# A list scheduler that ranks ready operations by deadline: pool and gated linear attention layers on eight cores

## The reference

```python
def pool_mixer(h, w_in, w_grp, scale, w_out):
    u, z = jnp.split(h @ w_in, 2, axis=-1)
    ...
        pooled.append((cg - shifted) / cnt - uf[:, :, gi])       # trailing mean minus token
    y = jnp.einsum('blgc,gcd->blgd', t, w_grp).reshape(B, L, D_INNER)
    y = y * scale * jax.nn.silu(z)
    return y @ w_out

def gla_mixer(h, w_in, w_gate2, b_gate, head_norm, w_out):
    ...
    def step(S, inp):
        cum = jnp.cumsum(lab, axis=2)
        qe = qb * jnp.exp(cum)
        ke = kb * jnp.exp(-cum)
        att = jnp.where(mask, jnp.einsum('bhtd,bhsd->bhts', qe, ke), 0.0)
        o = jnp.einsum('bhts,bhse->bhte', att, vb) + jnp.einsum('bhtd,bhde->bhte', qe, S)
        ...
        S_new = jnp.exp(g_tot)[..., None] * S + jnp.einsum('bhsd,bhse->bhde', kd, vb)
        return S_new, o
    ...
    o = o * lax.rsqrt(jnp.mean(o * o, axis=-1, keepdims=True) + EPS)   # per-head RMSNorm
    y = o.astype(h.dtype) * jax.nn.silu(z)
    return y @ w_out
```

## Time and profile before

| | us |
|---|---|
| median of three runs | 1924.77 (1924.33 to 1927.77) |
| profiled execution, its own time | 1927.73 |
| its span, slowest core (core 5) | 1926.1 |
| spans of the eight cores | 1913.7 to 1926.1 |
| TensorE busy | 1858.0 (96%) |
| VectorE busy | 1316.6 (68%) |
| ScalarE busy | 1286.4 (67%) |
| GpSimd busy | 585.8 (30%) |

### The profile page before, as it was taken

The page is one execution under the profiler, slowest core; times in us unless marked ns, Lnnn a source line. Parts: engine busy times, 40 slices in busy tenths (PEclk is TensorE's granted clock), DMA queues, the critical chain, the costliest instruction groups (busy, mean ns, idle before and its releaser), DMA issues.

```text
span 1926.1 us, 45504 instructions; the slowest of 8 cores (1913.7 to 1926.1 us)
## 1 busy us (share of the span) xinstructions
PE 1858.0 (96%) x15676; PEld 1316.1 (68%) x15676; DVE 1316.6 (68%) x2159; ACT 1286.4 (67%) x2727; POOL 585.8 (30%) x733
## 2 busy tenths in 40 slices
PE   5999999999999999999999999998999999999996
PEld 3777777666777766676676767776667676666663
DVE  2855756786777676778765656568767767677777
ACT  4955454676677777668875555556767676766886
POOL 1658733221111111111136686332111111111111
PEclk9999999999999999999999999999999999999998
DMA  8440312444113121212542221225422221211112
GB/s 187 115 79 15 67 29 50 72 73 78 31 29 57 31 53 32 53 31 47 82 76 45 38 44 35 45 51 88 81 43 39 38 48 32 55 31 30 52 65 80
DMA packets 105537, 107.10 MB, mean 56 GB/s; under 512 B 90080, under 2 KB 92512, under 8 KB 98272
## 3 DMA queue, kind: packets, MB, share of 16 engines
q0 software_dynamic: 11856, 63.64, 18.6%
q1 hardware_dynamic: 93456, 40.56, 9.3%
HBM read 138.45 MB, written 8.39 MB: 76 GB/s over the span
## 4 chain that ended last, share of the span: by engine, by line
PE 87%; issue 3%; DMA 3%; ACT 3%; DVE 2%; POOL 1%; ACTq 0%; DVEq 0%; POOLq 0%; SPq 0%
PE ps L410 87%; DMA hnT<-hnb 2%; DMA W<-wpack 1%; DVE hnb L444 1%; POOL SA L449 1%; ACT hnb L438 1%; ACT sg L438 1%; ACT U L438 0%; ACT rstd L438 0%; PE ps L418 0%; POOL SB L449 0%; DVE h L444 0%; POOL o L449 0%; DVE h L449 0%; ACT gs L438 0%
## 5 line engine op out<-in xcount | busy, mean ns | idle before, releaser
L410 PE MATMUL ps<-hnT,W 128*128 128x256 bf16 (+1 forms) x9216 | 970.7, 263 | 9.7 <-DVE Y L449 3.3
L410 PEld LDWEIGHTS ps<-hnT,W 128*128 128x128 bf16 x9216 | 824.2, 98 | 142.2 <-issue 20.5
L449 POOL TENSOR_TENSOR o<-o 128x256 bf16<-128x256 bf16 (+3 forms) x264 | 148.0, 561 | 582.6 <-ACT o L438 552.9
L410 PE MATMUL ps<-W,yT 128*128 128x512 bf16 x1024 | 253.0, 381 | 7.8 <-DVE yT L449 7.0
L444 DVE SCALAR_TENSOR_TENSOR h<-ps,rs,h 128x512 f32<-128x512 f32 x256 | 191.0, 746 | 90.2 <-ACT rs L438 73.9
L410 PE MATMUL ps<-W,Y 128*128 128x512 bf16 x1024 | 238.9, 383 | 12.1 <-DVE Y L449 6.8
L410 PE MATMUL ps<-W,hnT 128*128 128x512 bf16 (+1 forms) x1088 | 246.6, 380 | 0.0
L449 POOL TENSOR_TENSOR SA<-U 128x1080 f32<-128x1080 f32 (+7 forms) x72 | 135.5, 1882 | 283.6 <-ACT U L438 168.4
L438 ACT ACTIVATE Sb<-S,el 128x512 bf16<-128x512 f32 x256 | 184.1, 719 | 48.3 <-DVE S L444 40.3
L449 DVE TENSOR_TENSOR h<-h,ps 128x512 f32<-128x512 f32 x256 | 173.4, 684 | 62.3 <-PE ps L410 55.8
L444 DVE SCALAR_TENSOR_TENSOR S<-S,el,ps 128x512 f32<-128x512 f32 x240 | 177.3, 739 | 32.5 <-PE ps L410 28.5
(11 more groups left out here) (84 smaller groups left out, 2115.4 us busy)
## 6 DMA issues: line engine op xcount, KB each, us to landing
W<-wpack POOLq DMA_DIRECT2D x55, 1024.0 KB, 8.4
h<-x SPq DMA_DIRECT2D x16, 512.0 KB, 7.8
out<-h SPq DMA_DIRECT2D x16, 512.0 KB, 2.7
W<-wpack POOLq DMA_DIRECT2D x10, 512.0 KB, 7.1
gbc<-gains SPq DMA_DIRECT2D x5, 512.0 KB, 5.1
kd<-ke SPq DMA_TRANSPOSE x128, 2.3
hnT<-hnb SPq DMA_TRANSPOSE x48, 3.1
wg<-wg2p POOLq DMA_DIRECT2D x8, 64.0 KB, 2.5
```

The source lines that it names most:

```text
L410: ins = e.matmul(o_, lhsT=l_, rhs=r_, start=st, stop=sp_)
L449: P.op(eng, lambda e: e.tensor_tensor(out=out_, in0=a, in1=b, op=op), reads, writes, dve_dur(n) if eng == "dve" else n * 1.75 + 150.0, 100.0)
```

## The change

`schedule()` becomes a loop of six rounds. Each round runs the old scheduler (now `list_schedule()`), keeps the priorities that gave the shortest modelled span, and then computes new ones. `deadlines()` goes backward through the program. For an operation that is not on TensorE it takes the earliest time at which one of its users must start, where a TensorE user must start when the round before started it; from that it takes off the semaphore latency, the tail and a transfer's time. For ScalarE, VectorE and GpSimd the new `prio` is this time less the operation's own duration; TensorE and SyncE keep program order. The first round is the old order. The arithmetic and the engines of all operations stay as they are. The file grows by 28 lines, so L438 of before is L466 after, L410 is L438, L444 is L472, L449 is L477.

```diff
     DMA_NS_PER_BYTE = 1.0 / 270.0
     DMA_FIX = 2200.0
     TR_FIX = 5000.0
+    ROUNDS = 6
 
     def __init__(self):
         self.ops = []
@@ -111,6 +112,33 @@
         return op
 
     def schedule(self):
+
+
+        best = None
+        for it in range(self.ROUNDS):
+            self.list_schedule()
+            if best is None or self.span < best[0]:
+                best = (self.span, [o.prio for o in self.ops])
+            self.deadlines()
+        for o, p in zip(self.ops, best[1]):
+            o.prio = p
+        self.list_schedule()
+
+    def deadlines(self):
+        ops = self.ops
+        late = [self.span] * len(ops)
+        for o in reversed(ops):
+            t = o.start if o.eng == "pe" else self.span
+            for u in o.users if o.eng != "pe" else ():
+                lat = 0.0 if o.eng == u.eng and o.sem is None else self.SEM
+                fix = 0.0 if o.sem is None else (self.DMA_FIX if o.chan == "bulk" else self.TR_FIX) + o.bytes * self.DMA_NS_PER_BYTE
+                t = min(t, late[u.i] - lat - o.tail - fix - (u.dur if u.eng != "pe" else 0.0))
+            late[o.i] = t
+        for o in ops:
+            if o.eng in ("act", "dve", "pool"):
+                o.prio = late[o.i] - o.dur
+
+    def list_schedule(self):
         ops = self.ops
         for o in ops:
             o.users = []
```

## The result

| | before | after |
|---|---|---|
| median of runs on the same chip, us | 1925.1 | 1914.68 |
| ratio, 95% interval | | 0.9935, 0.9908 to 0.9963 |
| profiled execution, its own time, us | 1927.73 | 1917.35 |
| its span, slowest core, us | 1926.1 (core 5) | 1915.8 (core 0) |

A forecast was written before the change was run, and what follows sets the result against it. TensorE was taken as the bound (87% of the chain), so order could win only where it stands still or runs below full clock. Terms -4.5 - 4.0 - 2.2 + 0.6 - 0.8 + 1.5 = -9.4 gave 1915.4 us, range 1907 to 1925.

The forecast's parts named there:

- (e): Tail: last o's square goes before a hnb, giving back part of the 2.58 us gap; -0.8 us.
- (a): Gap at 443.50 in the first pool-to-GLA turn: closes, -3.3, plus 1.2 of clock behind it; together -4.5 us.
- (b): Third and fourth gaps in both pool-to-GLA turns: shorter by 0.7 and 1.3 us per turn; -4.0 us in sum.
- (d): First two gaps of both pool-to-GLA turns: TensorE's glr block moves behind the second, +0.3 each; +0.6 us.
- (c): Turn from GLA to second pool layer: o's square before hnb, two projections moved, gap of 2.24 closes; -2.2 us.
- (f): Inside the two GLA layers: new waits from the changed order of VectorE and ScalarE; +1.5 us.
- R2: Rival: slower through the GLA layers, VectorE taking S updates or scans ahead of yT or h; 1930 us, chance 0.10.
- R1: Rival: nothing won, closed gaps return at the next wait because the DMA delivering hnT decides; 1924 us, chance 0.18.
- R3: Rival: the first pool-to-GLA turn, once closed, runs at 0.81 of the clock instead of 0.97; 1933 us, chance 0.02.

The follow-up runs named there:

- e1: The kernel before, run again with no edit; 1927.61 us, ratio 1.0008.
- e8: The kernel before, with its old order, and both edits of the weight-load times (second head's loads later, first head's earlier); 1905.86 us, ratio 0.9891.
- e12: The kernel before with both load-time edits, and deadline order only at the turn from first GLA to second pool layer and in the tail; 1895.26 us.
- e7: The kernel after with both edits of the weight-load times (second head's loads later, first head's earlier); 1894.43 us, ratio 0.9836.
- e4: The kernel before with deadline order only in the two turns from pool to GLA, program order elsewhere; 1924.7 us, ratio 0.9985.

## Why the prediction was right, and where it was not

The number held by luck: an error in the tail and an error in the turns had opposite signs. By its own steps:

**(e) The tail: the term that was mis-sized, -0.8 against -7.2.** The mechanism was the right one (squares and yT taken before work that can wait), but I priced one gap, the last, with one displaced hnb. The view that I had already read said that 15.5 of the last 46.1 us were idle, of which that gap was 2.58. The same 1368 matmuls from the last weight load to the end, in three pieces cut at the start of the output matmuls of the third last and the last tile, of before and of after:

```profile
1743.10:1902.94 159.84, 155.19 (x1317) 107.33 (x1316) 124.38 (x226) 124.03 (x277) 25.65 (x57) 1.00 0.17 55
1902.94:1915.45 12.51, 7.89 (x45) 3.90 (x45) 9.29 (x14) 8.28 (x21) 2.02 (x4) 0.86 0.21 84
1915.45:1926.10 10.65, 3.37 (x9) 0.81 (x9) 3.83 (x4) 2.12 (x6) 1.32 (x1) 0.68 0.24 98
```

```profile
1733.00:1887.38 154.38, 153.44 (x1318) 107.86 (x1317) 123.25 (x226) 123.66 (x276) 26.12 (x57) 1.00 0.18 56
1887.38:1898.88 11.50, 7.55 (x45) 3.45 (x45) 9.20 (x13) 8.12 (x20) 1.76 (x3) 0.85 0.23 93
1898.88:1908.90 10.02, 1.91 (x9) 0.70 (x9) 3.98 (x4) 2.71 (x10) 0.42 (x1) 0.72 0.26 105
```

Of the 7.1 us between the two, 5.5 are in the first piece, which I had not priced at all (159.84 to 154.38), 1.0 in the second, and 0.6 in the last, on which I had put my -0.8. Idle time of the first piece fell from 4.65 to 0.94 us. Its busy time fell by 1.75 as well, for the same matmuls at clock 1.00. Their own durations add up to the same, 368.4 and 368.3 us, so they overlap more in after: what was lost in before lay between matmuls, in waits too short to show as idle. What made them wait is open. The clock of the other two pieces is nearly the same in both kernels, and is not the cause. Two of the gaps that I passed over in before, each ended by an order on ScalarE or VectorE:

```profile
1889.00 1.05 PE L410 MATMUL ps<-hnT,W 128*128 128x128 bf16 x16 [1.46 <-ACT vb L438]
...
1902.94 1.02 PE L410 MATMUL ps<-W,yT 128*128 128x512 bf16 x4 [1.19 <-DVE yT L449]
```

**(a) The gap at 443.50: the 3.3 us came, the clock's 1.2 did not.** The gap is gone, and so is the half clock behind it; but the gap that grew has 0.50 for some 6.8 us, as long as the two stretches that before has in turn 1 (from 376.5 to 379.8 and the earlier trace rows), and the mean clock of the 100 us is 0.97 as before. From 60 to 1880 us the cores of before and e1 stood at 0.50 for 12.0 and 13.7 us as a mean, those of after for 17.9: the term has the wrong sign for the whole. The cause that I named was one of two. I wrote that hnb, waiting 3.50 us for a transfer, stood ahead of o's square, and that moving it closes the gap. That is so, but e8 closes it with the old order by having the transfer on time. I took a late transfer for granted and priced the order.

**(b) The third and fourth gap: -4.0 was too much.** In turn 1 they gave 1.7 and 0.3 instead of 0.7 and 1.3. In turn 2 they gave 1.5 (2.90 to 1.41) and 0.3 (1.48 to 1.20). The sum of 3.7 us is near the term; its split is not, and turn 2 lost it again, to what follows.

**(d) The first two gaps: +0.6 was the wrong size, and the wait that I feared came from the other side.** I named "hnT landing later because its hnb now comes later" as what would make the whole wrong, and gave it no price. In turn 1 the gaps were 1.30 and 2.65, together 3.95, and are 5.24: +1.3 where I had +0.3; 0.4 of it is the glr block that no longer runs between them, and for the rest I have no row. In turn 2 the gap before `W,Y` went from 2.62 (at 1316.81) to 4.19, and the wait of 2.46 us is new, because hnT does land later there, but not because hnb comes later: hnb and its transposes come earlier than before, and so fall into a load. Turn 2 is 2.2 us slower, where I had it 1.7 faster. The step that failed is that I followed SyncE's transposes only as far as the operation that they wait for, and never laid GpSimd's loads of the same stretch beside them, though the durations from 3.1 to 11.3 us stood in the same trace.

**(c) GLA to pool: near the right number by another way.** The stage reads 2.5 us less, but its neighbour ahead 2.3 more (two cores, with 415.4 and 416.5, make 1.0 of that), so after alone does not settle it. With the loads out of the way it does: the first turn, its GLA layer and this turn together take 737.8 us in e12 and 740.3 in e8, -2.5, where I had -2.2. Yet the gap of 2.24 was only replaced, by one of 2.26 a tile later, at just the place where I saw hnb go ahead of o's square and took a projection on TensorE for cover. What was gained is a wait for sz in the last head, which I had not looked at (before):

```profile
938.93 1.91 PE L410 MATMUL ps<-hnT,W 128*128 128x256 bf16 x16 [1.04 <-DVE sz L444]
```

e8 has it too (1.05), after and e12 have no gap there. The other part stands in the clock. In e8 the gap of 2.24 is followed by 3.9 us at 0.56, which is 3.9 x 0.44 = 1.7 us, in e12 the gap of 2.26 by 1.00. That does not follow from the order: a gap of 2.23 to 2.27 us stands here on every core of each run, and the next 4 us have a clock of 0.57 to 0.65 on three of the eight cores in before, three in e1, eight in e8, two in after, five in e7 and two in e12, and 1.00 on the others. Six cores more in e8 than in e12, at 1.7 us each, are some 1.3 of the 2.5 us (an estimate).

**(f) Inside the GLA layers: about right, and R2 is out.** Of the 545 us of the earlier trace rows TensorE now stands 3.2 instead of 4.6, 2.26 of them in that one gap. No gap by yT, h or S appears all through them. The second GLA layer reads 0.5 us more on every core; the first cannot be told from a shift of its border.

**The rivals.** R1, gaps that come back at the next wait because the DMA decides, was right for the turns: together with their GLA layers they gave 2.0 less in the first and 2.7 more in the second, which is +0.7, where I had -7.9 + 1.5 = -6.4 (e4, with the order in the turns alone, has -2.4 there against before and e1). It was wrong for the whole because of the tail. R3 did not come: in e7, the densest of all, the 100 us of turn 1 have TensorE at 98.02 us and the clock at 1.00, and the mean clock of its eight cores is 0.996 to 0.999, above before's 0.988 to 0.994. The 0.81 of the earlier trace rows belongs to one execution: from 60 to 1880 us it stands on cores 4 to 7 of before, in stretches of 3.7 to 8.9 us, and on no core of any other profiled execution here, e1 with the same kernel included. By the section "Seeing it yourself" of the Trainium skill's "TensorE: Matmul & The Clock Gate" a die with three cores on dense matmuls stays at 13/16 of the clock while the load lasts; none of the profiled executions shows that.

## What to carry to other kernels

Before pricing an order of instructions, lay the transfers of the stretch beside each other by issue and landing: a gap that names an engine can be a late transfer three steps back, and then moving the large load can be worth more than a new order (here 21 us against 10 to 12). Where a stage is known to be a third idle, price all of its gaps, and ask of each engine on the way whether it can use what another one gives it early. A sum that comes out right proves none of its terms; hold each against its own stage.

## What the runs showed of the hardware

A transposing transfer of 128 x 1024 that takes 3.1 us alone took 5 to 11 us in the turns of core 5 when it was issued 0.04 to 5.5 us behind a 1 MB load of another queue, and landed 0.8 to 2.2 us after that load (368.97 and 369.87 after 368.04; before, 370.72 after 369.76 and 398.88 after 397.89). Being issued just ahead did not save it either: 0.65 us ahead it took 5.7 us, and on core 0 of after one issued 0.33 us ahead (879.60) took 13.0 and landed with its load. The Trainium skill, "DMA: Bandwidth & Descriptors", section "Issuing engines are not separate DMA queues", says that transfers run on the same 16 engines and interleave, whichever engine issued them. The trace agrees that another queue does not keep them apart. It does not show a small transfer getting through between the parts of a large one: of the 705 counted above none landed ahead of its load.
